# Two full experts as one wide item each: token columns streamed past stationary weights

## The reference

```python
logits = h @ w_router + b_router
top_l, top_e = lax.top_k(logits, 2)
gates = jax.nn.softmax(top_l, axis=-1)
# each row goes to 2 of 8 experts; for expert e, on its rows:
y_e = (jax.nn.silu(x @ w1[e]) * (x @ w3[e])) @ w2[e]
# the two results of a row are added, each by its gate
```

## Time and profile before

| | |
|---|---|
| time, median of 3 runs | 1945.62 us (1945.17 to 1946.29) |
| profiled execution, first to last instruction (its span) | 1943.1 us |
| TensorE, weight loads, VectorE, ScalarE busy | 1800.4, 1437.7, 1506.6, 1198.8 us |
| read from memory | 574.79 MB, 298 GB/s over the span |
| granted TensorE clock, mean | 0.969 of 2.4 GHz |

### The profile page before, as it was taken

One profiled execution on the slowest core, in us unless ns is written; L12 is line 12 of the kernel. 1 busy time (PEld: TensorE's weight loads), 2 busy tenths in 40 slices (PEclk: granted clock), 3 DMA queues, 4 the chain that ended last, 5 costly groups with the idle time before them and its releaser, 6 DMA issues.

```text
span 1943.1 us, 26608 instructions
## 1 busy us (share of the span) xinstructions
PE 1800.4 (93%) x9702; PEld 1437.7 (74%) x9702; DVE 1506.6 (78%) x1568; ACT 1198.8 (62%) x1115; POOL 18.2 (1%) x73
## 2 busy tenths in 40 slices
PE   7898799999999788999999999999899999999996
PEld 4666479998887666778777787787667676776764
DVE  4768464555798589888788787887989989898995
ACT  2233144434456268767666677677878778777883
POOL 1000000000000000000000000000000000000000
PEclk8889799999899879999999999999999999999999
DMA  9578876555725169999899798998999999999990
GB/s 336 205 279 291 297 244 200 186 177 181 232 90 208 53 233 381 379 333 345 328 336 365 285 357 317 332 355 322 389 383 388 396 385 386 380 392 381 387 385 23
DMA packets 221529, 579.24 MB, mean 298 GB/s; under 512 B 10479, under 2 KB 73399, under 8 KB 221438
## 3 DMA queue, kind: packets, MB, share of 16 engines
q1 hardware_dynamic: 220429, 573.98, 80.9%
q0 software_dynamic: 1024, 4.25, 0.7%
HBM read 574.79 MB, written 4.35 MB: 298 GB/s over the span
## 4 chain that ended last, share of the span: by engine, by line
PE 67%; DVE 15%; issue 8%; ACT 7%; DMA 2%; DVEq 1%; ACTq 0%; SPq 0%; PEldq 0%
PE banks L961 18%; PE banks L491 14%; PE banks L949 13%; DVE w_lo L1892 9%; ACT w_hi L1272 4%; PE banks L772 3%; PE banks L919 3%; PE banks L792 2%; PE banks L905 1%; PE banks L865 1%; DMA ring<-in_ada_w_dram 1%; PE banks L883 1%; PE banks L547 1%; PE banks L567 1%; PE banks L530 1%
## 5 line engine op out<-in xcount | busy, mean ns | idle before, releaser
L1892 DVE TENSOR_TENSOR w_lo<-ring,w_hi 128x2048 fp32r<-128x2048 f32 x420 | 949.8, 2289 | 166.1 <-ACT w_hi L1272 166.1
L1272 ACT CAST w_hi<-ring 128x2048 fp32r<-128x2048 f32 x420 | 797.5, 1910 | 291.4 <-PE banks L961 174.2
L961 PE MATMUL banks<-w_hi,x_s 128*128 128x512 f32 x672 | 279.5, 416 | 43.4 <-DVE w_lo L1892 39.7
L949 PE MATMUL banks<-w_hi,g_buf 128*128 128x512 f32 x784 | 286.8, 406 | 9.6 <-DVE w_lo L1892 8.5
L961 PE MATMUL banks<-w_hi,x_m 128*128 128x512 f32 x896 | 288.7, 398 | 0.6 <-DVE w_lo L1892 0.6
L961 PE MATMUL banks<-w_lo,x_s 128*128 128x512 f32 x672 | 267.0, 397 | 0.0
L949 PE MATMUL banks<-w_lo,g_buf 128*128 128x512 f32 x560 | 221.2, 395 | 0.0
L1424 DVE TENSOR_TENSOR w_lo<-ring,w_hi 128x1024 fp32r<-128x1024 f32 x124 | 143.8, 1204 | 84.2 <-ACT w_hi L1093 83.3
L961 PEld LDWEIGHTS banks<-w_hi,x_s 128*128 128x128 f32 x672 | 127.1, 189 | 105.6 <-DVE w_lo L1892 75.8
L1093 ACT CAST w_hi<-ring 128x1024 fp32r<-128x1024 f32 x124 | 121.5, 1031 | 127.7 <-PE banks L491 54.8
L961 PEld LDWEIGHTS banks<-w_hi,x_m 128*128 128x128 f32 x896 | 168.3, 188 | 41.2 <-DVE w_lo L1892 1.0
(11 more groups left out here) (377 smaller groups left out, 2042.8 us busy)
## 6 DMA issues: line engine op xcount, KB each, us to landing
ring<-in_moe_w_dram SPq DMA_DIRECT2D x420, 1024.0 KB, 6.9
ring<-in_ada_w_dram SPq DMA_DIRECT2D x48, 1024.0 KB, 7.4
ring<-in_ffn_w_dram SPq DMA_DIRECT2D x30, 1024.0 KB, 5.4
ring<-in_attn_w_qkv_dram SPq DMA_DIRECT2D x12, 1024.0 KB, 10.1
ring<-in_conv_w_pw_dram SPq DMA_DIRECT2D x12, 1024.0 KB, 11.9
ring<-in_cache_k_dram SPq DMA_DIRECT2D x16, 512.0 KB, 8.0
ring<-in_cache_v_dram SPq DMA_DIRECT2D x16, 512.0 KB, 6.5
ring<-in_attn_w_o_dram SPq DMA_DIRECT2D x4, 1024.0 KB, 8.0
```

The source lines that it names most:

```text
L949: mm = pe.matmul(out_b[:, b, :], g, y, start=(p == 0 and t == 0 and i == 0), stop=(p == NCH - 1 and t == 2 * last + 1 and i == len(g_passe ...
L961: mm = pe.matmul(bk[:, b, :], x, y, start=(k == 0 and i == 0), stop=(k == KC - 1 and i == len(x_passes(k, hi, lo)) - 1), skip_group_check= ...
L1272: act.copy(w_unit(n)[0], ring[:, pos_of(n), :]).then_inc(ev("moe_hi_ready"), 1)
L1892: dve.tensor_tensor(lo, ring[:, pos_of(n), :], hi.bitcast(F32), ALU.subtract).then_inc(ev("moe_lo_ready"), 1)
```

## The change

The routing also finds the two experts with the most rows (`big_key`, `big_top`). Each of them becomes a fixed item behind the first small one, of up to 208 rows and up to 176 rows (`BIG`); what is left over, and all other experts, go through the list as before, and the items of the list are numbered two later (`FIXED`). For a big item the units are cut in another way (`BIG_SLOTS`, 42 again): a w1 or w3 unit is 256 columns for all 1024 rows, and its 128-column blocks are stationary while the gathered tokens, 208 or 176 columns with the tokens along the columns, move past, in three separate passes. The products then stand the right way for w2, so nothing is turned; silu, product and split go over 2 x 208 or 2 x 176 numbers a partition. In a w2 unit the tokens are stationary as before, the first 128 in one block and the other 80 or 48 in a second one; the 48 have their high and low parts in one block of 96. The result of a second block has its own rows (`out_second`), gates (`gs_second`) and matmuls in `y_part`; all items behind the big ones do these too, with gates set to zero. The gather delivers tokens along the columns straight away (`gather`: for each of 8 chunks, high and low part, three matmuls that move the 208 or 176 columns of the selection matrix), without transposes; the gather for the large item behind the big ones is made in this way too, with 128. Several buffers move into others that are free by then.

```diff
+BIG = (208, 176)
+WIDE = max(BIG)
+FIXED = 1 + len(BIG)
+GROUPS = FE // 256
+BEHIND = 2
+def second_rows(b):
+    n = BIG[b] - P
+    return 2 * n if n <= SMALL else n
+def big_slots():
+    slots = []
+    for j in range(GROUPS + BEHIND):
+        if j < GROUPS:
+            slots += [("w1", j), ("w3", j)]
+        if j >= BEHIND:
+            slots.append(("w2", j - BEHIND))
+    return slots
+BIG_SLOTS = big_slots()
+assert len(BIG_SLOTS) == ES
+Y_BIG_AT = (1, 3)
+BIG_GATE_AT, BIG_NEXT_AT = 10, 13
+TAIL = ES - BEHIND - 1
...
+            def gather(width, chunks, at):
+                for k in chunks:
+                    for s, h in enumerate((h_tok_hi, h_tok_lo)):
+                        for i, (t0, tn) in enumerate(TILES):
+                            mm = pe.matmul(at(k)[:, s * width:(s + 1) * width], h[i][0:tn, k * P:(k + 1) * P], sel_m[0:tn, i, 0:width],
+                                           start=(i == 0), stop=(i == 2), skip_group_check=True)
+                return mm
+            def gather_big(b, part, first_bank):
+                pe.wait_ge(ev("big_sel_ready"), b + 1)
+                if part:
+                    pe.wait_ge(ev("big_x_ready"), 2 * b + 1)
+                mm = gather(BIG[b], range(4 * part, 4 * part + 4), lambda k: banks[:, first_bank + k % 4, :])
+                mm.then_inc(ev("big_x_filled"), 1)
...
+            def y_part(w, part, second=0, counted=0):
 
                 if part == 0:
                     pe.wait_ge(ev("moe_out_kept"), w + 1)
                     pe.wait_ge(ev("moe_gs_kept"), w + 1)
                     pe.wait_ge(ev("moe_y_zeroed"), 1)
+                    if counted:
+                        pe.wait_ge(ev("big_second_kept"), counted)
                 else:
                     pe.wait_ge(ev("moe_y_added"), 4 * w + 2)
                 for k in range(4 * part, 4 * part + 4):
-                    mm = pe.matmul(y_bank(k), out_sb[:, k * P:(k + 1) * P], gs[:, :], start=True, stop=True)
+                    mm = pe.matmul(y_bank(k), out_sb[:, k * P:(k + 1) * P], gs[:, :], start=True, stop=(second == 0))
+                    if second:
+                        mm = pe.matmul(y_bank(k), out_second[0:second, k * P:(k + 1) * P], gs_second[0:second, :], start=False, stop=True)
                 mm.then_inc(ev("moe_y_filled"), 1)
...
+            def big_unit(b, w, n, between=None):
+                kind, j = BIG_SLOTS[n]
+                width = BIG[b]
+                count = GROUPS * b + j
+                pe.wait_ge(ev("moe_lo_ready"), ES * w + n + 1)
+                hi, lo = w_unit(n)
+                if kind == "w2":
+                    pe.wait_ge(ev("big_g_lo_ready"), count + 1)
+                    if j == 0:
+                        pe.wait_ge(ev("moe_y_added"), 4 * w)
+                    g = big_g(b, j)
+                    def rows_of_first(t, h):
+                        c = slice(t * D + h * 512, t * D + (h + 1) * 512)
+                        first, first_low = g[:, t, 0:P], g[:, t, 2 * width - P:2 * width]
+                        for i, (x, y) in enumerate(((first, hi), (first, lo), (first_low, hi))):
+                            mm = pe.matmul(banks[:, 4 + h, :], x, y[:, c], start=(j == 0 and t == 0 and i == 0),
+                                           stop=(j == GROUPS - 1 and t == 1 and i == 2), skip_group_check=True)
+                        return mm
+                    def rows_of_second(t, h):
+                        c = slice(t * D + h * 512, t * D + (h + 1) * 512)
+                        rows = second_rows(b)
+                        if rows > width - P:
+                            passes = ((g[:, t, P:P + rows], hi), (g[:, t, P:P + rows], lo))
+                        else:
+                            second, second_low = g[:, t, P:width], g[:, t, width:width + rows]
+                            passes = ((second, hi), (second, lo), (second_low, hi))
+                        for i, (x, y) in enumerate(passes):
+                            mm = pe.matmul(banks[0:rows, 6 + h, :], x, y[:, c], start=(j == 0 and t == 0 and i == 0),
+                                           stop=(j == GROUPS - 1 and t == 1 and i == len(passes) - 1), skip_group_check=True)
+                        return mm
+                    for t in range(2):
+                        for h in range(2):
+                            mm = rows_of_second(t, h)
+                    if j == GROUPS - 1:
+                        mm.then_inc(ev("big_second_filled"), 1)
+                    for t in range(2):
+                        if t == 1 and between is not None:
+                            between()
+                        for h in range(2):
+                            mm = rows_of_first(t, h)
+                else:
+                    at = 0 if kind == "w1" else 2
+                    if j:
+                        pe.wait_ge(ev("big_silu_ready" if kind == "w1" else "big_g_ready"), count)
+                    hi, lo = (x.rearrange("p (k n) -> p k n", k=KC) for x in (hi, lo))
+                    for m in range(2):
+                        c = slice(m * P, (m + 1) * P)
+                        for k in range(KC):
+                            x, x_low = x_big[b][:, k, 0:width], x_big[b][:, k, width:2 * width]
+                            for i, (y, z) in enumerate(((hi, x), (lo, x), (hi, x_low))):
+                                mm = pe.matmul(banks[:, at + m, 0:width], y[:, k, c], z, start=(k == 0 and i == 0),
+                                               stop=(k == KC - 1 and i == 2))
+                mm.then_inc(ev("moe_units_used"), 1)
...
+                        def between():
+                            pe.wait_ge(ev("big_x_ready"), 2 * b + 4)
+                            big_gate_rows(b, w)
+                        big_unit(b, w, n, between)
+                    else:
+                        big_unit(b, w, n)
+                    if n in Y_BIG_AT:
+                        y_part(w - 1, Y_BIG_AT.index(n), second_rows(b - 1) if b else 0, b)
+                    if n == TAIL:
+                        pe.wait_ge(ev("big_silu_ready"), GROUPS * (b + 1))
+                        pe.wait_ge(ev("big_g_ready"), GROUPS * (b + 1))
+                        if last:
+                            gather_large()
+                        else:
+                            gather_big(b + 1, 0, 0)
+                    if n == TAIL + 1:
+                        if last:
+                            pe.wait_ge(ev("large_x_ready"), 2)
+                            big_gate_rows(b, w)
+                        else:
...
+                for n in range(ES):
+                    if b == 0 or n >= WBUF:
+                        cast(w, n)
+                    if n == WBUF - 1:
+                        keep_out(w - 1)
+                    kind, j = BIG_SLOTS[n - WBUF] if n >= WBUF else ("", 0)
+                    if kind == "w1":
+                        used(w, n - WBUF)
+                        if j:
+                            act.wait_ge(ev("big_g_ready"), GROUPS * b + j)
+                        act.activation(lit, banks[:, 0:2, 0:width], ACT.Silu).then_inc(ev("big_silu_ready"), 1)
+                    if kind == "w3":
+                        act.wait_ge(ev("big_g_ready"), GROUPS * b + j + 1)
+                        act.copy(big_g(b, j)[:, :, 0:width], product).then_inc(ev("big_g_hi_ready"), 1)
+                if last:
...
+            step(dve.scalar_tensor_tensor(big_key[:, :], cnt[:, :], 8.0, iota_e[:, :], ALU.mult, ALU.subtract))
+            settle()
+            step(dve.max(big_top[:, :], big_key[:, :]))
+            settle()
+            for b in range(2):
...
+            each_tile = big_oh[:, :, :].unsqueeze(2).to_broadcast([P, 2, 3, NE])
+            for term, value in ((0, rank_w), (1, gate_w)):
+                step(dve.tensor_tensor(big_terms[term], each_tile, value[:, :, 0:NE].unsqueeze(1).to_broadcast([P, 2, 3, NE]), ALU.mult))
+            step(dve.tensor_tensor(big_terms[2][:, :, 0, :], big_oh[:, :, :], iota_e[:, :].unsqueeze(1).to_broadcast([P, 2, NE]), ALU.mult))
+            step(dve.tensor_scalar(big_off[:, :], big_oh[:, 0, :], float(BIG[0]), None, ALU.mult))
+            settle()
+            step(dve.tensor_reduce(big_rank[:, :, :], big_terms[0], AX.X, ALU.add))
...
+            def select_big(b):
+                if b:
+                    dve.wait_ge(ev("big_x_filled"), 2 * b)
+                for i in range(3):
+                    last = dve.tensor_scalar(sel_m[:, i, 0:BIG[b]], iota_slot[:, 0:BIG[b]], big_rank[:, b, i:i + 1], None, ALU.is_equal)
+                last.then_inc(ev("big_sel_ready"), 1)
...
+                for n in range(ES):
+                    kind, j = BIG_SLOTS[n - WBUF] if n >= WBUF else ("", 0)
+                    count = GROUPS * b + j + 1
+                    if kind == "w3":
+                        dve.wait_ge(ev("moe_units_used"), ES * w + n + 1)
+                        dve.wait_ge(ev("big_silu_ready"), count)
```

(80 more changed lines are left out.)

250 lines of the change are left out of this document (172 added, 78 removed).

## The result

The changed kernel takes 1963.03 us (median of five runs, 1958.67 to 1968.15) where the kernel before takes 1946.29 beside it: a ratio of 1.008 [1.0058, 1.0101], slower by 0.8%. The forecast of 1928 was wrong in sign; the time lies at the upper edge of the range. The profiled execution spans 1960.1 us, 17.0 more than before.

A forecast was written before the change was run, and what follows sets the result against it. TensorE was taken to bound large and big items, the stream of weights small ones. Terms: -510.2 (items gone) + 481.1 (big items) + 3 (first item) + 4 (large item) + 4 (end) = -18.1 us; forecast 1928, range 1895 to 1965.

The forecast's parts named there:

- The pass price: Big items' w1 and w3 passes: 0.110 us each at both 208 and 176 columns, 147.8 us an item.
- Shorter passes: Rival, 9%: big items' w1 and w3 passes get shorter with their width, 0.095 and 0.080 us; 1867 us.
- the dense spacing of 0.1216: Rival, 23%: big items' w1 and w3 passes take the dense stage's 0.1216 us at both widths; 1959 us.
- the fp32 form: Rival, 5%: one-pass matmuls under 256 columns in big items take the full fp32 form's time; 2547 us.
- the overflow: Rival, 2%: an expert exceeds its 208 or 176 rows and keeps another item; one more small item makes 2042 us.
- the sum's 0 for the four small items: Four small items: 4 us more TensorE work each fits into 8.6 us to spare, adding 0.
- the stream of weights bounds it: Small items: loading 42 weight units of 1 MB, 2.71 us each, sets the 113.9 us.
- if the cover is gone, +4 each: Small items: without spare time to hide the added TensorE work, each takes 4 us more.
- From 710 us on the ring hides the greater part: First small item: the ring of weight loads hides most of the longer gather, leaving +1.7 us (ends 0 and 5.7).
- the +3: First small item: added routing, delayed loads and longer gather together cost 3 us more.
- the 0.72 forecast: Big gathers: 0.33 + 0.39 us for each block of 128, 128 and 8 rows, 11.6 us for 16 blocks.
- The switch of stationary columns: Big items' w2 units: switching between 80 or 96 and 128 stationary columns costs 1 us an item (ends 0 to 7.9).

The follow-up runs named there:

- the second experiment: Changed kernel without the second rows' y matmuls in the items behind the big ones and at the end (output incomplete): 1945.12 us, ratio 0.9985.
- the third: Changed kernel with the loops over large and small items cut to the one and four passes these inputs need: 1955.26 us, ratio 1.0029.
- the first: Changed kernel with each gather doing all its 128-row matmuls first and the 8-row ones behind them: 1936.00 us, ratio 0.9931.
- sixth experiment: Changed kernel with 128-row gather matmuls first, and the second big item's second-row y done once, in its last unit: 1923.95 us, ratio 0.9875.
- fifth: Changed kernel with two weight loads a block in place of three in the big items' w1 and w3 units: 1919.91 us, ratio 0.9839.
- seventh: Changed kernel with 128-row gather matmuls first, the second big item's second-row y once, and two weight loads a block: 1883.45 us, ratio 0.9654.

## Why the prediction was wrong

**The pass price held.** The median from start to start is 0.112 us in both items (forecast 0.110, equal in both), and that the load sets it is shown above. One of the two rows that the 0.110 came from was luck, though: transposes with only 8 stationary columns start 0.109 us apart as well, so it isn't the load of 128 columns that their 0.109 measures; the 64-column matmuls were the row that counted. From the changed kernel's timeline:

```profile
64.50 1.04 PE L610 MATMUL banks<-ident,arena 128*8 128x128 f32 x8 [0.53 <-DVE arena L1818]
```

Shorter passes, the dense spacing of 0.1216, the fp32 form and the overflow all fell. The Trainium skill (TensorE: Matmul & The Clock Gate, section LDWEIGHTS (loading the stationary operand)) gives a load its columns divided by 1.2 GHz, by which 107 ns is the estimate for 128; the trace agrees to 5%. The passes take 150.3 and 150.1 us, 4.7 more than forecast, of the 35 us missed. And the change lost with a pass well under the 0.1167 us that were to decide it.

**The step that failed most is the sum's 0 for the four small items: they took 13.9 us more.** It rested on "the stream of weights bounds it", read from a DMA share of 1.00, and on 8.6 us of idle TensorE. Half the bytes changed nothing, and TensorE's work reappeared in the item's length. After the change, a small item's lowerings are 1.8 us late at unit 6, behind the first y part, and 2.6 us late at unit 9, behind the second; from there the delay stays within 0.03 us to the item's end. Of the 3.6 us added 1.0 is hidden where it falls; of the delay nothing is made up. The chain shows how: cast, lowering and matmuls in series.

```profile
1590.84 1.88 PE banks L1038 x8
...
1592.74 1.92 ACT w_hi L1455
...
1594.69 2.30 DVE w_lo L2111
...
1597.04 2.13 PE banks L1038 x8
```

A cast waits for TensorE, the lowering for the cast, TensorE for the lowering: a closed loop through three buffers, in which what is added to any member while the others wait for it is not given back. The DMA share of 1.00 was the ring filled as fast as slots came free, no bound. The price that stood beside the 0, "if the cover is gone, +4 each", was nearer: 2.4 to 2.6 us each for the y, and the rest at the first of them. Here no y and no second rows (the second experiment) and loops without empty passes (the third) account for 11.0 and 2.5 of the 13.9 us.

**"From 710 us on the ring hides the greater part" failed too.** The order alone moved the first item by 9.0 us, more than the 7.2 us by which it went beyond the +3. The chain after runs through TensorE without a break from 706.74 to 735 us, where before it passed to ScalarE's casts at 714.91. The 1.7 us were judged by the DMA share again.

**Gathers were priced at full clock.** At full clock the block of 128, 128 and 8 rows cost 0.69 us at 208 columns and 0.66 at 176, a little under the 0.72 forecast; but the clock fell. At each of the big items' two ends it was at half for 13.7 us, in the first item for 10.2. That loses less than half of this time, for a 512-column pass goes from 0.233 to 0.427 us and a block from 0.66 to 1.10: set against the same rows at full clock, the gathers and w2 passes of the big items lost 11.5 us. The prediction named a clock of 1.00 in the big items as a sign, and at their ends it was 0.67. The sum there: 4.7 us (passes) and 11.5 (clock) more, and 8.6 less for the rest (seams, gathers at full clock, y, gate rows), which makes the 7.6 that TensorE's starts give. The switch of stationary columns, taken into the seams at 1 us, cost nothing; its upper price of 0.28 us came from no row, since the rows give 0.39 for a block.

**Empty loop passes were not in the sum.** The four more of them are 3.1 us at 0.77 each. In the first small item the long seam and the half clock behind it make 3.9 us of delay by unit 5, ahead of the y's 2.4. Of the end's +7.6, the second y makes 5.4 (forecast 4); the one more empty pass is the likely rest.

**What stays open:** why the clock falls at these gathers and not at the kernel before's, which have the same switch; the runs show only that it falls during long runs of 8-row blocks between 128-row ones and behind the idle seam, and that the order avoids it in two of three places (in the third it fell during the ordered run of 48). That the switches leave TensorE too thin, as the first expectation has it, was not tested by itself. A stretch at half clock from 708.1 to 711.5, ahead of the first gather, was not taken apart; such a stretch comes and goes from trace to trace (it is in the third and sixth experiment, not in the first, second, fifth and seventh), whatever the order, so some 1.5 us of the first item's 9.0 need not be the order's.

## What to carry to other kernels

A full DMA share, or idle time on an engine, is no proof of a bound or of cover: a loop of engines that wait for each other through few buffers passes on most of what is added to one of them (2.6 of 3.6 us here). Halving the bytes in one run shows whether the loads are the bound. Price a pass with stationary weights by its loads as well as by its columns, and let two passes share a load where they can. Work that is done with zeros "in all later items" is multiplied by them; do it once, where the data is made.

## What the runs showed of the hardware

- One-pass matmuls behind a load of 128 columns start 0.112 us apart at 176 and at 208 columns, and so do the records of fp32 ones of 8 columns; behind a load of 8 columns these start 0.025 us apart. Alternating with a pass of 416 or 352 columns, the pair takes 0.302 or 0.273 us, the long pass by its columns and the short one by its load.
- Second blocks of 80 or 96 stationary columns between 128-column ones cost nothing: twelve take 2.78 us, like the 2.80 of the full ones. A change in stationary rows, 128 to 8, does: at full clock eight blocks of 128, 128 and 8 rows take 5.3 us (0.66 each at 176 columns), and the same 24 matmuls 2.81 in order.
- The granted clock fell to 0.50 while TensorE was busy for the whole stretch (21.00 of 21.00 us at a mean of 0.67). There a 512-column pass took 0.427 us where it takes 0.233 at 1.00.
